# A decoder trunk's first sub-layer: both modulation rows built as rows, their slabs split between two engines, and h formed by token before plain transposes

## The chip, the cores and the metric

The kernel runs on one core of a Trainium2 chip. The metric is the device time of one execution in microseconds (us), the median of the runs. The engines are named as in the profile: PE is TensorE (PEld its weight loads), DVE is VectorE, ACT is ScalarE, POOL is GpSimd and SP is SyncE, which here issues most transfers.

## What is computed

A trunk of two layers on 256 tokens of width 1024, each layer a half-step FFN, a hybrid mixer and another half-step FFN. The change touches only the first sub-layer's input, h:

```python
mod = jax.nn.silu(c) @ w_ada[i] + b_ada[i]
sh1, sc1, g1, ... = jnp.split(mod, 9, axis=-1)
h = rms_norm(x, norm_pre[i, 0]) * (1 + sc1) + sh1
y = swiglu_ffn(h, w_ffn_in[i, 0], w_ffn_out[i, 0])
x = x + 0.5 * g1 * rms_norm(y, norm_post[i, 0])
```

`sc1` (the scale) and `sh1` (the shift) are each a product of a vector of 1024 with a 1024x1024 piece of `w_ada`, the same for every token. All arithmetic keeps fp32 accuracy: a product of two fp32 matrices is three products of their high and low parts.

## The kernel before

**Weights.** A chunk of weights is 128x1024 fp32 (512 KB). SP loads it into `w_raw` (8 buffers), ACT rounds it to `w_hi` (L1218), DVE subtracts to get `w_lo` (L1527), and PE multiplies: for each chunk of the first FFN 12 matmuls of 128x512 (L717, L718, L710), each preceded by a weight load. SP may load a chunk into a buffer once PE has used the one before (`w_used`).

**The first FFN's order.** FIRST_ORDER (L75) runs the first six chunks, numbered 0 to 5, with the first feature half of h alone (features 0 to 511, for three units of the hidden width); from chunk 6 the second half is needed. So the prologue makes h in two halves, and chunks 0 to 5 run on PE while the second half is made.

**Slabs.** `w_ada`'s pieces for scale and shift are 16 slabs of 128x1024 (`ada_slab_first`), in feature halves and loaded by SP in pairs: scale first half (signals `ada_first_landed0` to `3`), shift first half (`8` to `11`), then chunks 0 to 2, then scale second half (`4` to `7`), shift second half (`12` to `15`) with chunks 3 and 4 between, then the other chunks. A slab is used up either by DVE (a "step", L1555: accumulator plus slab times a column of silu(c), 128x512, counted in `ada_first_used`) or by PE (a matmul of the slab with that column broadcast). What DVE accumulates is 128 partial sums for each feature, with the bias in row 0; a matmul with ones sums them over the partitions and leaves the row in every partition of PSUM.

**Before, first half.** PE makes the whole scale row (L862 with ones, L866 for all 8 slabs). DVE turns it into AROW = (1 + scale) * norm_pre (L1566), multiplies x by it for each token tile (L1576) and makes a diagonal of 1/rms for each (L1666). h is then formed transposed, straight in two PSUM banks, as a sum of matmuls of 128x128 blocks: the first two shift slabs (L883), x times the diagonal (L894), and the accumulated rest of the shift times ones (L901), which waits for DVE's steps 0 to 5 on the shift. ACT rounds the result to `h_hi` (L1290), DVE subtracts to `h_lo` (L1586). PE's chunk 0 waits for `h_hi` of both token tiles and for `w_lo`.

**Before, second half.** DVE's steps 6 to 13 are the scale's 8 slabs, ended by a row of ones on PE ahead of chunk 3 (L874); steps 14 to 21 are the shift's 8 slabs. PE does the products of x with the diagonal ahead of chunk 4 and the shift's products with ones ahead of chunk 5. DVE's program between is `split_to` (the `w_lo` of a chunk) and `first_steps` in the order of L1997 to L2022.

**Beside it.** SP's load of the next sub-layer's `norm_pre` row (`pre_row`, L607) waits for `late_x`, and the bias load behind it waits until POOL has zeroed an accumulator, which waits until the second half of h is complete in PSUM (`t_ps`, L2055). Chunk 12's load stands behind both in SP's queue.

Of the kernel before, what the change touches and what calls it, by code (L numbers as in the profile page):

```python
# [11 lines left out]
ALU = mybir.AluOpType  # L12
AX_X = mybir.AxisListType.X

P = 128
D = 1024
# [251 lines left out]
def build(nc, x_d, c_d, w_ada, b_ada, norm_pre, norm_post, w_ffn_in, w_ffn_out, w_in, pool_w, w_ret_out, w_pool_out,  # L268
          w_ssm_out, w_fox_out, w_out, vecs_d, consts_d, out_d):
    with ExitStack() as ctx:  # L270
# [49 lines left out]
        DG, dg_off = sb("rstd_diagonal", [P, TT, P])  # L320
# [102 lines left out]
        first_a_ps = sem("first_half_scale_row_in_psum")  # L423
# [268 lines left out]
        def _(pe):  # L692
# [166 lines left out]
            def first_scale_row():  # L859

                pe.wait_ge(bias_landed[1].sem, bias_landed[1].at(0, 16))
                mm(PS[:, 4, :], ones, part(1)[:, 0:HALF], start=True, stop=False)  # L862
                for k in range(KD):
                    if k % 2 == 0:
                        pe.wait_ge(ada_first[k // 2], 16)
                    ins = mm(PS[:, 4, :], CS[:, k:k + 1].to_broadcast([P, P]), PSLAB[:, k, 0:HALF], start=False,  # L866
                             stop=(k == KD - 1))
                ins.then_inc(first_a_ps, 1)

            def late_scale_row():  # L870

                pe.wait_ge(first_used, FIRST_SCALE)
                pe.wait_ge(hl_ok.sem, hl_ok.at(0, 2))
                mm(PS[:, 6, :], ones, part(1)[:, HALF:D], start=True, stop=True).then_inc(a_ps.sem, 1)  # L874

            def first_pair_of_shifts():

                pe.wait_ge(ada_first[8], 16)
                pe.wait_ge(xsq_ok.sem, xsq_ok.at(0, 4))
                for tt in range(TT):  # L880
                    for k in range(4):
                        for i in range(2):
                            mm(PS[:, 6 + tt, k * P:(k + 1) * P], PSLAB[:, 8 + i, k * P:(k + 1) * P],  # L883
                               CS[:, i:i + 1].to_broadcast([P, P]), start=(k == 0 and i == 0), stop=False)

            def first_turn(half, tt):
# [5 lines left out]
                for k in range(4):  # L892
                    cs = slice(half * HALF + k * P, half * HALF + (k + 1) * P)
                    mm(PS[:, 6 + tt, k * P:(k + 1) * P], Y[:, tt, cs], DG[:, tt, :], start=(half == 1 and k == 0), stop=False)  # L894
# [1288 lines left out]
```

## Time and profile before

| | us |
|---|---|
| median of 3 runs | 1529.02 (1527.85 to 1530.41) |
| the profiled execution | 1528.89 |
| its span | 1527.1 |
| PE busy in the span | 1494.6 (98%) |
| DVE busy in the span | 1134.3 (74%) |
| granted TensorE clock, mean | 0.998 |

The span goes from the first instruction to the last, and 1.8 us of the execution lie around it. PE's share of busy time is an average: its idle time lies almost wholly in the first 50 us and in the sub-layers' boundaries. What the change touches lies in the first 55 us, so the profile is read there instruction by instruction.

### The profile page before, as it was taken

What the parts mean: (1) busy time and instruction counts of PE and PEld (TensorE: products, weight loads), DVE (VectorE), ACT (ScalarE), POOL (GpSimd) and SP (SyncE); (2) the same over time, 40 slices, a digit from 0 to 9 for tenths busy, and PEclk for the clock granted to TensorE, in tenths of its full rate; (3) what the DMA queues carried; (4) which work ended last, traced back from release to release, by engine and by line L of the source; (5) the groups of instructions that cost most, each with busy time, mean ns of one, the idle gap of its engine ahead of it and who ended that gap; (6) DMA issues with size and microseconds to landing.
All of it is one profiled execution on the core that took longest, in us unless ns stands there. A gap on an engine that the chain in (4) does not pass through costs nothing.

```text
span 1527.1 us, 20258 instructions
## 1 busy us (share of the span) xinstructions
PE 1494.6 (98%) x7904; PEld 1270.3 (83%) x7904; DVE 1134.3 (74%) x1337; ACT 780.8 (51%) x969; POOL 165.6 (11%) x96
## 2 busy tenths in 40 slices
PE   7999999999999999999999999999999999999998
PEld 4788888998988887888878888799989888878886
DVE  5887867867897988677677677767878979775453
ACT  3444455556473456444464444654746545554443
POOL 0000002203411110000000000040324012000000
PEclk9999999999999999999999999999999999999999
DMA  9899866655677856788767887565567777556652
GB/s 353 282 301 296 312 213 210 179 152 180 208 247 236 269 183 213 253 271 277 241 199 252 280 270 252 174 191 157 165 205 228 243 246 249 163 184 187 186 191 96
DMA packets 199779, 343.44 MB, mean 225 GB/s; under 512 B 18546, under 2 KB 109938, under 8 KB 199684
## 3 DMA queue, kind: packets, MB, share of 16 engines
q1 hardware_dynamic: 181540, 276.08, 57.2%
q10 hardware_dynamic: 18144, 66.07, 13.2%
q8 instruction: 62, 1.02, 0.3%
q14 instruction: 33, 0.27, 0.0%
HBM read 341.05 MB, written 1.05 MB: 224 GB/s over the span
## 4 chain that ended last, share of the span: by engine, by line
PE 83%; DVE 10%; issue 2%; ACT 2%; DMA 2%; SPq 0%; POOL 0%; ACTq 0%; DVEq 0%; POOLq 0%
PE ps L717 16%; PE ps L710 16%; PE ps L718 16%; PE ps L796 5%; PE ps L794 5%; PE ps L795 5%; PE ps L1156 4%; PE ps L1158 4%; PE ps L1157 4%; DVE w_lo L1527 2%; DVE ada_acc L1543 1%; PE ps L752 1%; DVE ada_acc L1555 1%; DMA w_raw<-in_w_ffn_in 1%; DMA ada_slab_first<-in_w_ada 1%
## 5 line engine op out<-in xcount | busy, mean ns | idle before, releaser
L1527 DVE TENSOR_TENSOR w_lo<-w_raw,w_hi 128x1024 fp32r<-128x1024 f32 x480 | 612.2, 1297 | 121.2 <-ACT w_hi L1218 120.2
L1218 ACT ACTIVATE w_hi<-w_raw 128x1024 fp32r<-128x1024 f32 x490 | 506.7, 1053 | 338.0 <-DMA w_raw<-in_w_ffn_in 114.0
L717 PE MATMUL ps<-w_hi,h_hi 128*128 128x512 f32 x1004 | 398.0, 396 | 4.2 <-DVE w_lo L1527 3.2
L718 PE MATMUL ps<-w_lo,h_hi 128*128 128x512 f32 x1004 | 391.8, 390 | 0.0
L710 PE MATMUL ps<-w_hi,h_lo 128*128 128x512 f32 x1004 | 389.8, 391 | 0.7 <-DVE h_lo L1683 0.6
L717 PEld LDWEIGHTS ps<-w_hi,h_hi 128*128 128x128 f32 x1004 | 189.0, 188 | 45.1 <-DVE w_lo L1527 4.6
L710 PEld LDWEIGHTS ps<-w_hi,h_lo 128*128 128x128 f32 x1004 | 188.3, 188 | 42.6 <-DVE h_lo L1683 2.5
L718 PEld LDWEIGHTS ps<-w_lo,h_hi 128*128 128x128 f32 x1004 | 189.1, 188 | 37.5
L1156 PE MATMUL ps<-h_hi,w_hi 128*128 128x256 f32 x704 | 201.6, 286 | 0.0
L1157 PE MATMUL ps<-h_lo,w_hi 128*128 128x256 f32 x704 | 199.1, 283 | 0.0
L1158 PE MATMUL ps<-h_hi,w_lo 128*128 128x256 f32 x704 | 199.1, 283 | 0.0
L1543 DVE SCALAR_TENSOR_TENSOR ada_acc<-ada_slab,c_silu,ada_acc 128x1024 f32<-128x1024 f32 x128 | 187.2, 1462 | 4.6 <-DMA ada_slab<-in_w_ada 4.6
L794 PE MATMUL ps<-w_hi,act_hi 128*128 128x512 f32 x352 | 137.6, 391 | 0.0
L795 PE MATMUL ps<-w_lo,act_hi 128*128 128x512 f32 x352 | 137.0, 389 | 0.0
L796 PE MATMUL ps<-w_hi,act_lo 128*128 128x512 f32 x352 | 137.0, 389 | 0.0
L1156 PEld LDWEIGHTS ps<-h_hi,w_hi 128*128 128x128 f32 x704 | 134.9, 192 | 1.6 <-DVE w_lo L1527 0.4
L1157 PEld LDWEIGHTS ps<-h_lo,w_hi 128*128 128x128 f32 x704 | 135.0, 192 | 0.3
L1158 PEld LDWEIGHTS ps<-h_hi,w_lo 128*128 128x128 f32 x704 | 135.0, 192 | 0.0
L1727 DVE TENSOR_TENSOR act_by_token<-gate_silu,ps 128x512 f32<-128x512 f32 x44 | 30.2, 687 | 133.8 <-PE ps L710 117.9
L2044 POOL MEMSET ada_acc<- 128x1024 f32 x18 | 17.0, 954 | 649.6 <-PE ps L847 601.4
L1336 ACT ACTIVATE gate_silu<-ps 128x512 f32<-128x512 f32 x44 | 26.3, 598 | 118.7 <-PE ps L710 118.7
L796 PEld LDWEIGHTS ps<-w_hi,act_lo 128*128 128x128 f32 x352 | 66.1, 188 | 13.9
(283 smaller groups left out, 1657.9 us busy)
## 6 DMA issues: line engine op xcount, KB each, us to landing
w_raw<-in_w_ffn_in SPq DMA_DIRECT2D x352, 256.0 KB, 3.6
w_raw<-in_w_in SPq DMA_DIRECT2D x168, 512.0 KB, 3.6
ada_slab<-in_w_ada ACTq DMA_DIRECT2D x126, 512.0 KB, 4.5
w_raw<-in_w_ffn_out SPq DMA_DIRECT2D x88, 512.0 KB, 4.3
ada_slab_first<-in_w_ada SPq DMA_DIRECT2D x16, 512.0 KB, 8.8
w_raw<-in_w_ssm_out SPq DMA_DIRECT2D x16, 512.0 KB, 4.4
w_raw<-in_w_out SPq DMA_DIRECT2D x16, 512.0 KB, 3.4
w_raw<-in_w_pool_out SPq DMA_DIRECT2D x8, 512.0 KB, 3.7
```

Source lines behind the costliest of these rows:

```text
L710: return mm(PS[:, banks + tt, :], lo[:, k, tok(tt)], wh[:, kk * HALF:(kk + 1) * HALF], start=False, stop=(k == kn - 1))
L717: mm(out, hi[:, k, tok(tt)], wh[:, cs], start=(k == 0), stop=False)
L718: mm(out, hi[:, k, tok(tt)], wl[:, cs], start=False, stop=False)
L794: mm(out, hi[:, k, tok(tt)], wh[:, cs], start=first, stop=False)
L795: mm(out, hi[:, k, tok(tt)], wl[:, cs], start=False, stop=False)
L796: return mm(out, lo[:, k, tok(tt)], wh[:, cs], start=False, stop=last)
L1156: mm(out, wh[:, cs], HH[:, k, :], start=(k == 0 and t % 2 == 0), stop=False)
L1157: mm(out, wh[:, cs], HL[:, k, :], start=False, stop=False)
L1158: ins = mm(out, wl[:, cs], HH[:, k, :], start=False, stop=(k == KD - 1 and t % 2 == 1))
L1218: fn(WH[:, n % N_HI, 0:width], RAW[:, n % N_RAW, 0:width], ACT.Copy).then_inc(w_hi, 1)
L1527: dve.tensor_tensor(WL[:, n % N_RAW, 0:width], RAW[:, n % N_RAW, 0:width], WH[:, n % N_HI, 0:width], ALU.subtract).then_inc(w_lo, 1)
L1543: dve.scalar_tensor_tensor(part(n), slab, CS[:, k:k + 1], part(n), ALU.mult, ALU.add)\
```

## The change

The first half's scale row is now made half by PE (slabs 0 to 3) and half by DVE (slabs 4 to 7, steps 0 to 3), with ones last. The first half's shift becomes a row as well, with DVE on slabs 0 to 3 (steps 4 to 7) and PE on slabs 4 to 7. With both rows in PSUM, DVE forms h by token, `Y = Y / rms + shift` (`first_h_full`), and PE makes 4 plain transposes for each token tile. The diagonal is gone. In the second half the scale row stays as it was; the shift row is made by DVE for slabs 0 to 5 and by PE for slabs 6 and 7, and everything that follows it (h by token, transposes) now stands ahead of chunk 6. SP's queue is as before. The core of the diff:

```diff
-FIRST_STEPS = [(1, 0, k) for k in range(2, 8)] + [(0, 1, k) for k in range(8)] + [(1, 1, k) for k in range(ADA_FIRST)]
-FIRST_SHIFT, FIRST_SCALE, LATE_SHIFT = 6, 14, 22
+FIRST_STEPS = [(0, 0, k) for k in range(4, 8)] + [(1, 0, k) for k in range(4)] + [(0, 1, k) for k in range(8)]
+FIRST_STEPS += [(1, 1, k) for k in range(6)]
+FIRST_SCALE, FIRST_SHIFT, LATE_SCALE, LATE_SHIFT = 4, 8, 16, 22
...
+            def first_row(n, half, bank, slabs, steps):
+
+                cs = slice(half * HALF, (half + 1) * HALF)
+                for k in slabs:
                     if k % 2 == 0:
+                        pe.wait_ge(ada_first[8 * n + 4 * half + k // 2], 16)
+                    mm(PS[:, bank, :], CS[:, k:k + 1].to_broadcast([P, P]), PSLAB[:, 8 * n + k, cs], start=(k == slabs[0]),
+                       stop=False)
+                pe.wait_ge(first_used, steps)
+                return mm(PS[:, bank, :], ones, part(PARTS[n])[:, cs], start=(not slabs), stop=True)
...
+                    ins = pe.transpose(PS[:, 6 + tt, k * P:(k + 1) * P], Y[:, tt, half * HALF + k * P:half * HALF + (k + 1) * P],
+                                       ident)
...
                     if s == 0 and c == 3:
-                        late_scale_row()
-                    if s == 0 and c in (4, 5):
+                        pe.wait_ge(hl_ok.sem, hl_ok.at(0, 2))
+                        first_row(0, 1, 6, (), LATE_SCALE).then_inc(a_ps.sem, 1)
+                    if s == 0 and c == 2 * EARLY:
+                        first_row(1, 1, 7, (6, 7), LATE_SHIFT).then_inc(first_rows, 1)
                         for tt in range(TT):
-                            (first_turn if c == 4 else first_shifts)(1, tt)
+                            first_turn(1, tt)
...
-            first_scale_row()
-            first_pair_of_shifts()
+            first_row(0, 0, 4, (0, 1, 2, 3), FIRST_SCALE).then_inc(first_rows, 1)
+            first_row(1, 0, 5, (4, 5, 6, 7), FIRST_SHIFT).then_inc(first_rows, 1)
+            pe.wait_ge(ident_landed, 16)
...
+            def first_h_full(half):
+
+                cs = slice(half * HALF, (half + 1) * HALF)
+                dve.wait_ge(first_rows, 2 + half)
+                for tt in range(TT):
+                    dve.scalar_tensor_tensor(Y[:, tt, cs], Y[:, tt, cs], RB[:, tt:tt + 1], PS[:, 5 + 2 * half, :], ALU.mult,
+                                             ALU.add).then_inc(late_x if half else f_ok.sem, 1)
```

On PE at the program's start, before (names: `ada_acc` is DVE's accumulator, `small_columns` holds the ones, `c_silu` the column of silu(c)):

```order
L862 MATMUL ps<-ada_acc,small_columns 128x512 [waits ada_bias_landed1,c_silu_ready,ones_ready]
L866 MATMUL ps<-ada_slab_first,c_silu 128x512 [waits ada_first_landed0]
...
L866 MATMUL ps<-ada_slab_first,c_silu 128x512 [waits ada_first_landed3]
L866 MATMUL ps<-ada_slab_first,c_silu 128x512
L883 MATMUL ps<-c_silu,ada_slab_first 128x128 [waits x_squared,ada_first_landed8]
L883 MATMUL ps<-c_silu,ada_slab_first 128x128 x15
L894 MATMUL ps<-rstd_diagonal,y_tok 128x128 [waits x_scaled_ready]
...
L901 MATMUL ps<-small_columns,ada_acc 128x128 [waits ada_first_used]
```

The same place in the changed kernel (`consts` holds the identity):

```order
L865 MATMUL ps<-ada_slab_first,c_silu 128x512 [waits ada_first_landed1]
L865 MATMUL ps<-ada_slab_first,c_silu 128x512
L868 MATMUL ps<-ada_acc,small_columns 128x512 [waits ada_first_used]
L865 MATMUL ps<-ada_slab_first,c_silu 128x512 [waits ada_first_landed10]
L865 MATMUL ps<-ada_slab_first,c_silu 128x512
L865 MATMUL ps<-ada_slab_first,c_silu 128x512 [waits ada_first_landed11]
L865 MATMUL ps<-ada_slab_first,c_silu 128x512
L868 MATMUL ps<-ada_acc,small_columns 128x512 [waits ada_first_used]
L877 MATMUL ps<-consts,y_tok 128x128 [waits x_scaled_ready,identity_landed]
L877 MATMUL ps<-consts,y_tok 128x128 x3
```

Eight slab matmuls of the scale became four, the 32 small matmuls of shift and diagonal went, and between the two rows PE now waits for the shift's last two slab pairs.

On PE around chunk 6, the changed kernel (the L710 row ends chunk 5, the L717 row begins chunk 6):

```order
L710 MATMUL ps<-w_hi,h_lo 128x512
L865 MATMUL ps<-ada_slab_first,c_silu 128x512 [waits ada_first_landed15]
L865 MATMUL ps<-ada_slab_first,c_silu 128x512
L868 MATMUL ps<-ada_acc,small_columns 128x512 [waits ada_first_used]
L877 MATMUL ps<-consts,y_tok 128x128 [waits second_half_x_scaled]
L877 MATMUL ps<-consts,y_tok 128x128 x3
L877 MATMUL ps<-consts,y_tok 128x128 [waits second_half_x_scaled]
L877 MATMUL ps<-consts,y_tok 128x128 x3
L717 MATMUL ps<-w_hi,h_hi 128x512 [waits w_lo_split,h_lo_ready]
```

Before, nothing stood between chunks 5 and 6; the second half's matmuls stood one and two chunks earlier (L894 ahead of chunk 4, L901 ahead of chunk 5).

On DVE for the same stretch, before, from the `w_lo` of chunk 4 to that of the chunks from 6 on:

```order
L1527 TENSOR_TENSOR w_lo<-w_raw,w_hi 128x1024 [waits w_hi_split]
L1555 SCALAR_TENSOR_TENSOR ada_acc<-ada_slab_first,c_silu,ada_acc 128x512 [waits ada_first_used,ada_bias_landed0,ada_first_landed14] x2
L1555 SCALAR_TENSOR_TENSOR ada_acc<-ada_slab_first,c_silu,ada_acc 128x512 [waits ada_first_used,ada_bias_landed0,ada_first_landed15] x2
L1527 TENSOR_TENSOR w_lo<-w_raw,w_hi 128x1024 [waits ada_first_used,w_hi_split]
L1586 TENSOR_TENSOR h_lo<-ps,h_hi 128x4x128 [waits h_hi_ready] x2
```

And in the changed kernel:

```order
L1506 TENSOR_TENSOR w_lo<-w_raw,w_hi 128x1024 [waits w_hi_split]
L1534 SCALAR_TENSOR_TENSOR ada_acc<-ada_slab_first,c_silu,ada_acc 128x512 [waits ada_first_used,ada_bias_landed0,ada_first_landed13]
L1534 SCALAR_TENSOR_TENSOR ada_acc<-ada_slab_first,c_silu,ada_acc 128x512 [waits ada_first_used,ada_bias_landed0,ada_first_landed14] x2
L1506 TENSOR_TENSOR w_lo<-w_raw,w_hi 128x1024 [waits ada_first_used,w_hi_split]
L1564 SCALAR_TENSOR_TENSOR y_tok<-y_tok,small_columns,ps 128x512 [waits first_rows_in_psum]
L1564 SCALAR_TENSOR_TENSOR y_tok<-y_tok,small_columns,ps 128x512
L1573 TENSOR_TENSOR h_lo<-ps,h_hi 128x4x128 [waits h_hi_ready] x2
L1506 TENSOR_TENSOR w_lo<-w_raw,w_hi 128x1024 [waits w_hi_split] x6
```

Two operations that wait for PE's new row were put in, and the `w_lo` of chunk 6 stays behind them and behind `h_lo`.

## Rows read from the trace of the kernel before

**Rows 1.** The page's first part: busy time and share of each engine.

```profile
PE 1494.6 (98%) x7904; PEld 1270.3 (83%) x7904; DVE 1134.3 (74%) x1337; ACT 780.8 (51%) x969; POOL 165.6 (11%) x96
```

**Rows 2.** Timeline, 7 to 20 us (start, duration, instruction, idle before); L866's durations.

```profile
7.83 2.04 PE L862 MATMUL ps<-ada_acc,small_columns 128*128 128x512 f32 x2 [7.83 <-DMA ada_acc<-in_b_ada]
L866 PE MATMUL ps<-ada_slab_first,c_silu x16: 592/592/1061, 9.7 to 17.4; 128*128 128x512 f32 x16
10.58 0.16 DVE L1617 SCALAR_TENSOR_TENSOR small_columns<-small_columns 128x1 f32<-128x1 f32 x1
17.67 0.75 DVE L1555 SCALAR_TENSOR_TENSOR ada_acc<-ada_slab_first,c_silu,ada_acc 128x512 f32<-128x512 f32 x1 [6.93 <-DMA ada_slab_first<-in_w_ada]
19.24 0.68 DVE L1566 SCALAR_TENSOR_TENSOR scale_row<-ps,scale_row 128x512 f32<-128x512 f32 x1
```

**Rows 3.** SP's issues (timeline), each followed by its DMA row, us to landing.

```profile
4.76 0.48 SPq L626 DMA_DIRECT2D ada_slab_first<-in_w_ada  x1
ada_slab_first<-in_w_ada SPq DMA_DIRECT2D x1, 512.0 KB, 7.5
...
5.80 0.45 SPq L632 DMA_DIRECT2D scale_row<-in_norm_pre  x1
scale_row<-in_norm_pre SPq DMA_DIRECT2D x1, 256.0 KB, 9.2
...
7.68 0.48 SPq L626 DMA_DIRECT2D ada_slab_first<-in_w_ada  x1
ada_slab_first<-in_w_ada SPq DMA_DIRECT2D x1, 512.0 KB, 11.2
...
8.21 0.79 SPq L626 DMA_DIRECT2D ada_slab_first<-in_w_ada  x1
ada_slab_first<-in_w_ada SPq DMA_DIRECT2D x1, 512.0 KB, 12.0
```

**Rows 4.** Timeline, 21 to 30 us, DVE and PE, up to chunk 0.

```profile
21.55 3.40 DVE L1555 SCALAR_TENSOR_TENSOR ada_acc<-ada_slab_first,c_silu,ada_acc 128x512 f32<-128x512 f32 x4
25.01 2.05 PE L901 MATMUL ps<-small_columns,ada_acc 128*128 128x128 f32 x16 [1.65 <-DVE ada_acc L1555]
27.75 0.50 PE L717 MATMUL ps<-w_hi,h_hi 128*128 128x512 f32 x1 [0.69 <-ACT h_hi L1290]
28.68 1.23 DVE L1527 TENSOR_TENSOR w_lo<-w_raw,w_hi 128x1024 fp32r<-128x1024 f32 x1 [0.26 <-ACT w_hi L1218]
```

**Rows 5.** Timeline, 37 to 55 us, from the second scale row to chunk 6.

```profile
37.73 1.12 PE L874 MATMUL ps<-ada_acc,small_columns 128*128 128x512 f32 x2 [0.29 <-DVE ada_acc L1555]
39.38 0.69 DVE L1566 SCALAR_TENSOR_TENSOR scale_row<-ps,scale_row 128x512 f32<-128x512 f32 x1 [0.56 <-PE ps L874]
44.63 1.22 DVE L1527 TENSOR_TENSOR w_lo<-w_raw,w_hi 128x1024 fp32r<-128x1024 f32 x1
45.90 0.50 PE L717 MATMUL ps<-w_hi,h_hi 128*128 128x512 f32 x1 [2.22 <-DVE w_lo L1527]
50.35 1.95 PE L901 MATMUL ps<-small_columns,ada_acc 128*128 128x128 f32 x16
52.96 0.69 DVE L1586 TENSOR_TENSOR h_lo<-ps,h_hi 128x512 fp32r<-128x512 f32 x1 [0.20 <-ACT h_hi L1290]
53.57 6.89 DVE L1527 TENSOR_TENSOR w_lo<-w_raw,w_hi 128x1024 fp32r<-128x1024 f32 x6
54.93 0.47 PE L717 MATMUL ps<-w_hi,h_hi 128*128 128x512 f32 x1
```

**Rows 6.** Windows: us, then PE, PEld, DVE, ACT, POOL busy, granted clock, DMA share, GB/s.

```profile
25.00:27.70 2.70, 2.05 (x16) 1.86 (x16) 1.78 (x2) 1.20 (x3) 0.00 (x0) 1.00 1.07 401
45.90:50.40 4.50, 4.50 (x13) 3.54 (x14) 3.95 (x5) 0.00 (x0) 0.00 (x0) 0.62 1.03 371
60.00:200.00 140.00, 140.00 (x639) 115.68 (x638) 114.53 (x109) 66.81 (x75) 2.87 (x3) 1.00 0.91 307
```

**Rows 7.** Timeline at 63 us: four plain transposes, of an FFN unit.

```profile
63.20 0.60 PE L752 MATMUL ps<-consts,act_by_token 128*128 128x128 f32 x4
```

More of the change, by code:

```diff
@@ L892, in first_turn @@
                 for k in range(4):
-                    cs = slice(half * HALF + k * P, half * HALF + (k + 1) * P)
-                    mm(PS[:, 6 + tt, k * P:(k + 1) * P], Y[:, tt, cs], DG[:, tt, :], start=(half == 1 and k == 0), stop=False)
-            def first_shifts(half, tt):
-                pe.wait_ge(first_used, FIRST_SHIFT if half == 0 else LATE_SHIFT)
-                for k in range(4):
-                    cs = slice(half * HALF + k * P, half * HALF + (k + 1) * P)
-                    ins = mm(PS[:, 6 + tt, k * P:(k + 1) * P], part(0)[:, cs], ones, start=False, stop=(k == 3))
+                    ins = pe.transpose(PS[:, 6 + tt, k * P:(k + 1) * P], Y[:, tt, half * HALF + k * P:half * HALF + (k + 1) * P],
+                                       ident)
                 ins.then_inc(t_ps.sem, 1)
@@ L1424, in mixer @@
                     if c == 1 and layer == 0:
+                        act.wait_ge(ident_landed, 16)
                         fn(SEL[0:32, :], ident[0:32, 0:20], ACT.Copy)
@@ L1562, in first_scale_row @@
                 if half == 0:
-                    dve.wait_ge(first_a_ps, 1)
+                    dve.wait_ge(first_rows, 1)
                 else:
@@ L1571, in first_scale_row, with first_x_scale @@
                     chain(ins)
-            def first_x_scale(half, tt):
+            def first_x_scale(half):
                 cs = slice(half * HALF, (half + 1) * HALF)
-                ins = dve.tensor_tensor(Y[:, tt, cs], X[:, tt, cs], AROW[:, cs], ALU.mult)
-                if half:
-                    ins.then_inc(late_x, 1)
+                for tt in range(TT):
+                    ins = dve.tensor_tensor(Y[:, tt, cs], X[:, tt, cs], AROW[:, cs], ALU.mult)
+                chain(ins)
+            def first_h_full(half):
+                cs = slice(half * HALF, (half + 1) * HALF)
+                dve.wait_ge(first_rows, 2 + half)
+                for tt in range(TT):
+                    dve.scalar_tensor_tensor(Y[:, tt, cs], Y[:, tt, cs], RB[:, tt:tt + 1], PS[:, 5 + 2 * half, :], ALU.mult,
+                                             ALU.add).then_inc(late_x if half else f_ok.sem, 1)
             def first_h_lo(half):
@@ L1999, in _ @@
             x_root(0, 1)
-            first_steps(0, 2)
+            first_steps(0, FIRST_SCALE)
             first_scale_row(0)
-            for tt in range(TT):
-                first_x_scale(0, tt)
-                first_diagonal(tt)
-            first_steps(2, FIRST_SHIFT)
+            first_x_scale(0)
+            first_steps(FIRST_SCALE, FIRST_SHIFT)
+            first_h_full(0)
             split_to(0)
@@ L2021, in _ @@
             split_to(5)
+            first_h_full(1)
             first_h_lo(1)
```

41 lines of the change are left out of this document (7 added, 34 removed).

## The prediction

> **What bounds the kernel now.** I read the page's first part, then the timeline of the first 55 us, then windows for the stretch behind it. PE is busy 98% of the span [rows 1] and without a gap from 60 to 200 us [rows 6], so once chunk 6 starts, a shift of its start moves everything behind it by as much. The question is when chunk 6 starts: 54.93 us before [rows 5]. Up to there PE is not the bound. Four places set the pace: the first shift slabs' landing, for which DVE idled 6.93 us [rows 2]; h_hi ahead of chunk 0, at 27.75 [rows 4]; DVE's chain of steps and w_lo, which released chunk 4 at 45.90 after PE had idled 2.22 us; and chunk 4, the shift's products (50.35) and chunk 5, back to back on PE, up to 54.93 [rows 5].
>
> **The unit prices.** A DVE step starts 0.88 us behind the one before (4 steps in 3.40 us [rows 4], one alone 0.75 [rows 2]). A w_lo takes 1.15 us of DVE's time (6 in 6.89) [rows 5]. An fp32 matmul of 128x512 is two passes: two passes to the end of the result took 1.12 us at the high clock [rows 5] and 2.04 us at the low one [rows 2], hence, with the drain taken off, about 0.43 and 0.86 us a pass. A chunk takes 2.8 us at the high clock: chunk 5 lies between L901's end, drain taken off (52.1), and 54.93 [rows 5].
>
> **Part 1, the scale row of the first half.** x's roots are done at 10.74 [rows 2]. DVE then runs four steps; the last slab pair landed at 4.76 + 7.5 = 12.3 us [rows 3], so they end between 14.2 and 15.0. PE has 8 passes from about 7.9, the first ones slow as before, and waits; the ones take 1.12. AROW's own input lands at 5.80 + 9.2 = 15.0 [rows 3]. The scale row's DVE operation starts at about 15.6, instead of 19.24 [rows 2]: 3.6 us earlier, since it no longer stands behind two steps that wait for slabs. The x products follow (1.3 us) and four steps on the shift (3.5), done by about 21.
>
> **Part 2, the shift row, where that gain goes.** PE's half of the shift is slabs 4 to 7, the last to arrive: 7.68 + 11.2 = 18.9 and 8.21 + 12.0 = 20.2 us [rows 3]. From 18.9 it has 8 slab passes and 2 of ones, 4.3 us at the high clock, with a short wait for the last pair: done at 23.4. But PE has stood idle from about 15.4 to 18.9. In the trace, chunk 4 came after 2.22 us of idle time [rows 5] and ran with a granted clock of 0.62 over 4.5 us [rows 6], that is, 3.4 us at the low level (1.2 GHz) and the rest at 2.4; 1.65 us of idle time ahead of L901 [rows 4] did not lower it (1.00 afterwards) [rows 6]. An idle time of 3.5 us is beyond the row that lowered it, so I take the low clock and its 3.4 us: 1.7 us lost, shift row done at 25.2. The bounds are 23.4 and, were all 10 passes slow, 27.5.
>
> Then DVE forms h of both tiles (0.3 to see the row, the nearest rows being 0.1 and 0.5; 0.69 and 0.6 for two operations such as L1566 [rows 5]), done at 26.8; 4 transposes take 0.60 [rows 7]; ACT's h_hi ends at 28.1. Chunk 0 starts at 28.15, against 27.75 [rows 4]: +0.4 (bounds: -1.4 and +2.7). Taking out the diagonal and 32 small matmuls is free, since PE waits there for DVE or slabs anyway.
>
> **Part 3, DVE's chain to chunk 4.** The w_lo of chunk 1 starts 0.45 later than 28.68. Up to the w_lo of chunk 4 the chain was DVE's: 12 steps, three more w_lo, the scale row and two products, and it ended at 45.85. Now it has 11 steps (-0.88) and one wait for the last product (+0.1): 45.5, a gain of 0.35. The products of x with the diagonal ahead of chunk 4 are gone from PE, which is worth nothing: PE waited 2.22 us behind them [rows 5], and now waits some 3.5. Chunk 4 therefore runs at the low clock as before (4.45 us, 45.90 to 50.35) and ends at 49.95, chunk 5 at 52.75.
>
> **Part 4, ahead of chunk 6.** Before, the shift's products cost PE 1.70 us on the path, and all that followed them (h_hi, h_lo, the w_lo of chunk 6) ran beside chunk 5. Now the row stands behind chunk 5 and covers nothing:
> - 2 slabs and the ones: 6 passes and the drain, 2.85 us, to 55.6;
> - DVE sees it and forms h of both tiles: 1.6, to 57.2;
> - 4 transposes of the second tile: 0.65, to 57.85;
> - from there to PE's release, as from L901's end (52.30) to 54.85 in the trace, h_hi, h_lo and the w_lo of chunk 6: 2.55 [rows 5], to 60.4.
> Against 54.93 chunk 6 starts **5.5 us later**. The w_lo of chunks 6 on stood in the same queue before, behind h_lo; they were merely hidden.
>
> **Part 5, the clock behind it.** Of 55.6 to 60.4 PE works 1.2 us at most, on transposes, and then idles 2.5 us at a stretch. By the row with 2.22 us the clock falls: 3.4 us at the low level cost 1.7 more. The other bound is nothing, by the row with 1.65 us.
> Of transposes the traces before show no case of their own. The Trainium skill ("TensorE: Matmul & The Clock Gate", Part 4: PE-mode transpose) says that transposes do not count as busy for the clock. Its rule makes the idle stretch longer and the fall surer; without it I would take the same value with less weight.
>
> **Part 6, queues.** late_x now comes from h by token, so SP's norm_pre row, the bias and then chunk 12's load are issued near 59 instead of 53.6, some 1.3 us nearer to chunk 6 than before. Chunk 12 is wanted 16 us after chunk 6; that room hides it, and costs nothing. POOL's zeroing moves along.
>
> **The sum.** +5.5 and +1.7 on the profiled execution's 1528.89, which lies at the median of the runs (1529.02): **1536.1**.
>
> **The rivals.**
> 1. One of the two new low stretches fails to come (the clock depends on where the idle time falls, and either place has two stretches of work near it). Without the one behind chunk 5: 1534.4. Without the one in the shift row the start moves by -1.8, and all behind it: 1534.3.
> 2. Neither comes: 1532.6. For it speaks only that 1.65 us were harmless; against it, that both gaps are above 2.22.
> 3. Not slower: the clock stays high in chunk 4 too. It decides there: if the new 3.5 us gap ahead of chunk 4 falls so that the clock does not drop, or drops after chunk 5, the old loss of 1.7 us goes as well, and with rival 2 the sum is 5.5 - 1.8 - 1.7 = +2.0: 1530.9, within 0.2%. Against it: chunk 4's gap grows.
> 4. The low clock lasts longer: all ten passes of the shift row (+2.3), or also chunk 5 (+1.4): 1538.
> 5. The change doesn't hold chunk 6 back at all, because the second half's row is made while PE waits for chunk 4's w_lo. PE runs its program in order and the row stands behind chunk 5, and DVE's last steps end at about 48: it can't, unless the order is not what it reads. It would give the start's -0.35 and the 1.7 of the shift's products: 1526.8.
>
> **The numbers.** Forecast 1536.1 with 0.47; rival 1 0.26; rival 2 0.08; rival 3 0.07; rival 4 0.09; rival 5 0.03. The range takes in rivals 1 and 2 and most of 4: 1532.3 to 1538.2. About 0.2% (3.06 us) is what a measurement of this kernel tells from no change. Slower by more than that: the forecast, rivals 1 and 4, most of rival 2: 0.86. Within: 0.11. Faster: 0.03.
>
> **What would show it.** In the changed kernel's timeline: the first scale row's DVE operation near 15.6; a PE gap up to 18.9, then slab passes with a granted clock near 0.5 to 0.6; chunk 0 at 28.2 (26.4 if that clock is high); chunk 4 near 45.5; the second shift row ending near 55.6, and PE's next L717 near 60.4, with a low granted clock in the 3 us behind it. I am wrong if chunk 6 starts before 58, if the shift row isn't the last input of chunk 0, or if PE is idle again between 60 and 200 us, which would let a later start be made up.

## The result, and the profile after

The changed kernel takes **1540.20 us** (median of 4 runs, 1538.75 to 1544.68), the kernel before in the same comparison 1528.43 us (4 runs, 1527.28 to 1530.41). The ratio is 1.0081, with a 95% interval of 1.0070 to 1.0093: slower. A second comparison gave 1537.95 against 1528.14, 1.0060 (1.0043 to 1.0077). The profiled execution is one of 1538.75 us with a span of 1536.9.

The page's first part for the changed kernel (busy us, share, records of each engine) answers to [rows 1]. PE has 72 records fewer (a record is one pass of a matmul, and an fp32 matmul has two), and as many weight loads fewer. That looked like nothing, and is what the second half of this text is about.

```profile
PE 1495.6 (97%) x7832; PEld 1265.1 (82%) x7832; DVE 1135.7 (74%) x1339; ACT 781.6 (51%) x969; POOL 165.6 (11%) x96
```

Timeline of the changed kernel, 13 to 28 us, PE and DVE up to chunk 0; it answers to [rows 2, 4]:

```profile
15.93 0.69 DVE L1545 SCALAR_TENSOR_TENSOR scale_row<-ps,scale_row 128x512 f32<-128x512 f32 x1 [1.29 <-PE ps L868]
...
18.43 5.40 PE L865 MATMUL ps<-ada_slab_first,c_silu 128*128 128x512 f32 x8 [2.62 <-DMA ada_slab_first<-in_w_ada]
...
23.67 1.02 PE L868 MATMUL ps<-ada_acc,small_columns 128*128 128x512 f32 x2
...
24.73 1.40 DVE L1564 SCALAR_TENSOR_TENSOR y_tok<-y_tok,small_columns,ps 128x512 f32<-128x512 f32 x2 [3.34 <-PE ps L868]
...
27.53 0.50 PE L717 MATMUL ps<-w_hi,h_hi 128*128 128x512 f32 x1 [0.69 <-ACT h_hi L1268]
```

Timeline of the changed kernel, 43 to 60 us, from chunk 4's `w_lo` to chunk 6; it answers to [rows 5]:

```profile
43.70 1.22 DVE L1506 TENSOR_TENSOR w_lo<-w_raw,w_hi 128x1024 fp32r<-128x1024 f32 x1
44.98 0.50 PE L717 MATMUL ps<-w_hi,h_hi 128*128 128x512 f32 x1 [2.87 <-DVE w_lo L1506]
...
51.68 1.88 PE L865 MATMUL ps<-ada_slab_first,c_silu 128*128 128x512 f32 x4
...
53.39 1.02 PE L868 MATMUL ps<-ada_acc,small_columns 128*128 128x512 f32 x2
...
54.45 1.41 DVE L1564 SCALAR_TENSOR_TENSOR y_tok<-y_tok,small_columns,ps 128x512 f32<-128x512 f32 x2 [5.72 <-PE ps L868]
55.25 1.31 PE L877 MATMUL ps<-consts,y_tok 128*128 128x128 f32 x8 [0.84 <-DVE y_tok L1564]
56.58 1.35 DVE L1573 TENSOR_TENSOR h_lo<-ps,h_hi 128x512 fp32r<-128x512 f32 x2 [0.72 <-ACT h_hi L1268]
...
59.20 0.47 PE L717 MATMUL ps<-w_hi,h_hi 128*128 128x512 f32 x1 [2.63 <-DVE w_lo L1506]
```

Windows of the changed kernel (columns as in [rows 6]; the seventh is the granted clock, 1.00 for 2.4 GHz): the shift row of the first half, chunk 4, and the stretch behind chunk 6's start.

```profile
20.00:25.00 5.00, 4.69 (x8) 1.64 (x6) 1.53 (x3) 1.06 (x1) 0.00 (x0) 0.69 1.07 396
44.00:48.00 4.00, 3.01 (x12) 2.17 (x12) 3.59 (x5) 0.00 (x0) 0.00 (x0) 1.00 1.08 384
60.00:64.00 4.00, 4.00 (x12) 3.14 (x11) 4.00 (x5) 3.98 (x5) 0.00 (x0) 0.59 0.76 234
```

The chain that the prediction described is there, row for row. Chunk 6 starts at 59.20 instead of 54.93 [rows 5], and the low clock behind it makes that 5.9 us at the first transposes of an FFN unit (69.11 instead of 63.20 [rows 7]). But the span grew by 9.8 us (1536.9 against 1527.1). The other 4 us came far behind the prologue, at the boundaries between sub-layers: 2.2 of them near 600 us. In the changed kernel ACT waits longer there for the load of a weight chunk, then PE for what ACT and DVE make behind that. ACT's row and PE's row of the kernel before near 600 us:

```profile
601.09 1.06 ACT L1218 ACTIVATE w_hi<-w_raw 128x1024 fp32r<-128x1024 f32 x1 [3.53 <-DMA w_raw<-in_w_ffn_in]
...
604.90 0.66 PE L752 MATMUL ps<-consts,act_by_token 128*128 128x128 f32 x4 [1.44 <-DVE act_by_token L1727]
```

The same two of the changed kernel:

```profile
609.03 1.06 ACT L1196 ACTIVATE w_hi<-w_raw 128x1024 fp32r<-128x1024 f32 x1 [5.20 <-DMA w_raw<-in_w_ffn_in]
...
612.85 0.66 PE L752 MATMUL ps<-consts,act_by_token 128*128 128x128 f32 x4 [2.02 <-DVE act_by_token L1709]
```

That longer idle time is 0.6 of the 2.2 us. The rest is a fall of the clock that came ahead of both rows, behind an idle time of PE that is shorter than at the same place before (1.36 against 1.65 us); the changed kernel's row, and its window behind it:

```profile
598.49 1.32 PE L835 MATMUL ps<-consts,y_tok 128*128 128x128 f32 x8 [1.36 <-DVE y_tok L1656]
600.00:604.00 4.00, 4.00 (x11) 3.15 (x12) 4.00 (x5) 3.40 (x4) 0.00 (x0) 0.57 0.09 15
```

### The profile page after: what moved, and what is told of

It reads as the page before. It is cut to its first block, busy times and chain, and to the rows that moved or that the text cites. A ratio compares the mean times of both kernels' runs of the same rounds, so it can differ in the third digit from the quotient of the medians.

```text
span 1536.9 us, 20118 instructions
## 1 busy us (share of the span) xinstructions
PE 1495.6 (97%) x7832; PEld 1265.1 (82%) x7832; DVE 1135.7 (74%) x1339; ACT 781.6 (51%) x969; POOL 165.6 (11%) x96
## 4 chain that ended last, share of the span: by engine, by line
PE 81%; DVE 11%; issue 3%; ACT 2%; DMA 2%; SPq 0%; POOL 0%; ACTq 0%; DVEq 0%; POOLq 0%
PE ps L717 16%; PE ps L710 15%; PE ps L718 15%; PE ps L795 5%; PE ps L796 5%; PE ps L794 5%; PE ps L1135 4%; PE ps L1137 4%; PE ps L1136 4%; DVE w_lo L1506 2%; DVE ada_acc L1522 1%; PE ps L752 1%; DMA w_raw<-in_w_ffn_in 1%; DVE x_res L1631 1%; DVE y_tok L1640 1%
## 5 line engine op out<-in xcount | busy, mean ns | idle before, releaser
L717 PE MATMUL ps<-w_hi,h_hi 128*128 128x512 f32 x1004 | 399.4, 398 | 8.2 <-DVE w_lo L1506 7.2
L710 PE MATMUL ps<-w_hi,h_lo 128*128 128x512 f32 x1004 | 391.0, 392 | 0.1
L717 PEld LDWEIGHTS ps<-w_hi,h_hi 128*128 128x128 f32 x1004 | 189.6, 189 | 50.2 <-DVE w_lo L1506 6.6
L710 PEld LDWEIGHTS ps<-w_hi,h_lo 128*128 128x128 f32 x1004 | 189.2, 189 | 42.2 <-DVE h_lo L1665 1.7
```

Of the source, the lines that this page charges most:

```text
L710: return mm(PS[:, banks + tt, :], lo[:, k, tok(tt)], wh[:, kk * HALF:(kk + 1) * HALF], start=False, stop=(k == kn - 1))
L717: mm(out, hi[:, k, tok(tt)], wh[:, cs], start=(k == 0), stop=False)
```

## The experiments

All ratios are against the kernel before, run in the same comparison, with 95% intervals.

### Is a later start of chunk 6 passed on in full?

The kernel before with useless fp32 matmuls of 128x512 between chunks 5 and 6 (N is 2, 4, 7 and 9):

```diff
+                    for _ in range(N):
+                        mm(PS[:, 6, :], ones, X[:, 0, 0:HALF], start=True, stop=True)
```

> The kernel before with 2 useless fp32 matmuls of 128x512 (ones times x, 4 passes) on PE between chunks 5 and 6: a pure delay of 1.7 us of all that follows, with PE busy. Theory A (what is lost ahead of chunk 6 is passed on one to one and nothing else happens): +1.7 us on the kernel before, mean granted clock as before (0.998). Theory B (the place in time of the later gaps decides whether PE's clock falls there, so that a mere shift can cost several us more): +1.7 and 0 to 6 us more, the surplus with a lower mean clock.

> The same with 4 useless matmuls: a delay of 3.4 us. Theory A: +3.4 us, clock as before. Theory B: +3.4 plus a surplus that differs from those of the delays of 1.7 and 6.0 us; since each low stretch in both traces lasts 3.4 us, the smallest surplus of the three is expected here.

> The same with 7 useless matmuls: a delay of 6.0 us, as much as the changed kernel lost up to 70 us. Theory A: +6.0 us, clock 0.998. Theory B: about what the changed kernel shows against before, +9 to +12, with a mean clock of 0.991 to 0.995.

> The kernel before with 9 useless matmuls between chunks 5 and 6, a delay of 7.7 us with PE busy, by which boundary gaps fall at the times at which they fall in the changed kernel. If the changed kernel's low-clock stretches behind 590 us come from where the gaps fall: +10 us or more with a mean clock of 0.996 or less. If not: +6.5 to +8 us, clock 0.998 or more.

| N | PE's added work, us | median, us | less before's | ratio |
|---|---|---|---|---|
| 2 | 1.7 | 1530.22 | +2.1 | 1.0011 (1.0001 to 1.0020) |
| 4 | 3.5 | 1532.22 | +4.1 | 1.0022 (1.0012 to 1.0031) |
| 7 | 6.1 | 1532.76 | +4.6 | 1.0032 (1.0021 to 1.0043) |
| 9 | 7.9 | 1536.00 | +7.8 | 1.0046 (1.0032 to 1.0060) |

(The added work is N times 0.877 us, from the last one's row of 18 records in 7.89 us.) Over the four, a delay in front of chunk 6 is passed on: the total is within 0.6 us of it for three and 1.5 us under it for N = 7, whose mean clock was the highest of the four (0.9989, the others 0.9972 to 0.9975). Nothing behind it adds to it, and the surplus of theory B did not come. So the changed kernel's +9.8 to +11.8 needs more than its prologue. That its time is real and no accident of one comparison:

> The changed kernel once more, beside the delays on the same chip. Both theories: +10 to +13 us on the kernel before with a mean clock of 0.991 to 0.995; by theory B its executions differ by their clock, 1 to 2 us for each 0.001 of it.

Measured: 1537.95 us, 1.0060 (1.0043 to 1.0077), +9.8 us, just under what was expected. Three of its four executions have a mean clock of 0.992 to 0.996; the fourth is listed with 0.944 and is the second fastest, so that reading is not used.

### Which half of the change costs what?

The second half's edit alone, on before's first half (the `late_shift_row` and the transposes ahead of chunk 6):

```diff
-                    if s == 0 and c in (4, 5):
+                    if s == 0 and c == 2 * EARLY:
+                        late_shift_row()
                         for tt in range(TT):
-                            (first_turn if c == 4 else first_shifts)(1, tt)
+                            late_turn(tt)
```

> Half of the change alone: the first half of h as before, the second half's shift as a row with h by token and transposes ahead of chunk 6. Theory 1 (the loss is the serial row, h, transposes, h_hi, h_lo and w_lo between chunks 5 and 6): chunk 6 starts near 60 us and is followed by a low-clock stretch, +7 to +11 us on the kernel before, as much as the whole change. Theory 2 (the first half's PE idle time and its low clock carry a good part of the loss): +3 to +5 us.

Measured: 1535.22 us, 1.0040 (1.0026 to 1.0055), +7.0 us, the low end of theory 1; chunk 6 at 60.34, behind the same idle time of 2.63 us.

The first half's edit alone, with before's second half (products with the diagonal ahead of chunk 4, the shift's ahead of chunk 5):

```diff
-                    if s == 0 and c == 2 * EARLY:
-                        first_row(1, 1, 7, (6, 7), LATE_SHIFT).then_inc(first_rows, 1)
+                    if s == 0 and c in (4, 5):
                         for tt in range(TT):
-                            first_turn(1, tt)
+                            (late_turn if c == 4 else late_shifts)(tt)
```

> The other half alone: both rows, h by token and transposes for the first half, the second half as before (all 8 shift slabs on DVE, products with the diagonal and with ones ahead of chunks 4 and 5). Theory 1: chunk 0 near 27.5, chunk 6 within 1 us of before, and the time within 1.5 us of the kernel before. Theory 2: +3 to +6 us.

Measured: 1529.16 us, 1.0001 (0.9990 to 1.0011), and chunk 6 at 54.16, 0.8 us earlier than before, without a gain in the total. The second half's edit carries the loss. The first half's, which starts chunk 6 earlier, should have gained and doesn't: its ten executions have a mean granted clock of 0.996, the kernel before's 0.998.

A rebuilt version keeps the first half by rows and takes the second half's row off the path: four slabs each on DVE and PE, PE's ahead of chunk 4 and the ones ahead of chunk 5, h by token beside chunk 5, the transposes ahead of chunk 5's last product, and chunk 6's `w_lo` ahead of `h_lo`.

```diff
+                    if s == 0 and c == 4:
+                        late_slabs((4, 5))
+                        late_slabs((6, 7))
+                    if s == 0 and c == 5:
+                        pe.wait_ge(first_used, LATE_SHIFT)
+                        mm(PS[:, 7, :], ones, part(0)[:, HALF:D], start=False, stop=True).then_inc(first_rows, 1)
```

> The changed kernel with its second half put where PE has room: slabs 4 to 7 of the shift on PE ahead of chunk 4 (DVE keeps 4 slabs), the row of ones ahead of chunk 5, the transposes inside chunk 5, and chunk 6's w_lo ahead of h_lo. Theory 1: the serial stretch is covered by chunk 5, PE is never idle for long behind 42 us, chunk 6 starts at 53 to 54 us: -2 to 0 us on the kernel before. Theory 2: +3 or more remains.

Measured: 1531.53 us, 1.0017 (1.0006 to 1.0028), although chunk 6 starts at 51.82, 3.1 us before it does in [rows 5]. The mechanism of the prologue was mended and the time was still above before's; again the mean clock was 0.996. Something in the two kernels with the first half by rows costs time far from it: by the median and the start of chunk 6 in the profiled execution, some 2 us in the first half's edit alone and some 6 in this one.

### The low clock

The changed kernel with three matmuls that add nothing (the stationary operand is zero) in the idle time ahead of chunk 6:

```diff
+                        for _ in range(3):
+                            mm(PS[:, 4, :], DA[:, 0, 0:1].to_broadcast([P, P]), X[:, 0, 0:HALF], start=False, stop=False)
```

> The changed kernel with three more fp32 matmuls of 128x512 on PE behind the second half's transposes and ahead of chunk 6. Their stationary operand is zero and they go into a bank that the units accumulate in, so they add nothing; PE would have idled there for 2.63 us behind h_hi, h_lo and the w_lo. Theory A, the low clock behind chunk 5 comes from that idle time: PE's idle time ahead of chunk 6 shrinks to under 0.3 us, chunk 6 starts within 0.2 us of where it did (59.2), the granted clock of 60 to 64 us is 1.00 instead of low, and the time falls by 1.7 us against the changed kernel, to about 1536.3 in these comparisons (ratio to the kernel before 1.005). Theory B, the clock falls there for another reason: it is low again between 60 and 64 and the time stays near 1538.

Timeline and window of that kernel: the filling leaves no idle time ahead of chunk 6, which starts where it did, and the clock stays high.

```profile
56.51 2.74 PE L905 MATMUL ps<-x_res,da 128*128 128x512 f32 x6
...
59.30 0.47 PE L717 MATMUL ps<-w_hi,h_hi 128*128 128x512 f32 x1
```

```profile
60.00:64.00 4.00, 4.00 (x20) 3.26 (x19) 4.00 (x5) 3.98 (x5) 0.00 (x0) 1.00 0.80 252
```

Twenty matmuls instead of twelve in the same 4 us, as by theory A. The time was 1536.93, 1.0044 (1.0031 to 1.0058), where 1.005 was expected. The same filling also in the gap between the first half's two rows:

```diff
             first_row(0, 0, 4, (0, 1, 2, 3), FIRST_SCALE).then_inc(first_rows, 1)
+            for _ in range(3):
+                mm(PS[:, 7, :], ones, PSLAB[:, 0, 0:HALF], start=True, stop=True)
```

> As the run before, and three more such matmuls (ones against a slab, into a bank that is written anew later) between the first scale row (done at 15.8) and the first shift slab that PE waits for (18.4). Theory A: the low stretch of the first shift row goes too, chunk 0 starts at 25.9 instead of 27.5, and the time is 3.4 us below the changed kernel's, near 1534.6; if the number of later low stretches follows from the early ones it may be lower still. Theory B, later low stretches are drawn anew in each execution and have nothing to do with the prologue: the mean clock rises only by the two early stretches. Theory C, the first stretch is low whatever PE did before: chunk 0 stays at 27.3 to 27.5.

Its trace has the shift row's slabs in 3.70 us instead of 5.40 and chunk 0 at 26.19 instead of 27.53. Its median, 1535.77 (1534.6 was expected), 1.0049 (1.0037 to 1.0062), is no better than that of the run before within the intervals, and the mean clock is 0.996 in both. So the fillings do what they should where they stand, and the clock far behind does not follow them.

Is it the first half by rows that brings the later low clock? Before's first half with the rebuilt version's second half (the diff is against the second half's edit alone), and the rebuilt version with the first gap filled, by the lines just shown:

```diff
-                    if s == 0 and c == 2 * EARLY:
+                    if s == 0 and c == 4:
+                        late_slabs((4, 5))
+                        late_slabs((6, 7))
+                    if s == 0 and c == 5:
                         late_shift_row()
-                        for tt in range(TT):
-                            late_turn(tt)
```

> The kernel before's first half with another second half: the shift as a row, four slabs on DVE and four on PE ahead of chunk 4, its row of ones ahead of chunk 5, h by token beside chunk 5, and the transposes ahead of that chunk's last product, with the w_lo of chunk 6 ahead of h_lo. If the extra low stretches that the kernels with the first half by rows showed far behind the prologue come from that first half, this one has a mean clock like the kernel before's (0.998 and more); chunk 6 starts near 52.5 to 53.5 and the time is 1526.5 to 1528, ratio 0.999 to 1.000. If they come with any second half that is early or by rows, it has them too: a mean clock of 0.995 to 0.997 and 1529 to 1531.

> The rebuilt version (both halves by rows, the second half as in the run before) with the three matmuls in the gap between the first scale row and the first shift slabs. With the first stretch at the high clock in each execution chunk 0 starts at 25.7 in each and chunk 6 near 51.8. If the early idle time of 3.5 us is what brings the later low stretches, the mean clock rises to 0.998 and more and the time falls to 1526 to 1527.5, below the kernel before; if the later ones are drawn independently, the time is at most 1 us under the 1531.5 of the rebuilt version.

Measured: 1527.76 us, 0.9995 (0.9986 to 1.0003), mean clock 0.9985 and chunk 6 at 53.43, for the first; 1531.22 us, 1.0014 (1.0005 to 1.0022), mean clock 0.9961, for the second. The extra loss goes with the first half by rows, and not with its idle time, which the second kernel doesn't have. What else goes with it is the number of PE's records: 14 fewer than before in the first of these two, 62 in the second, 54 and 68 in the first half's edit alone and the rebuilt version.

### What the boundaries show

The DMA view of one stretch lists the queues at work in it. For the kernel before, from SP's issue of the loads behind the boundary near 600 us (595.79) to ACT's use of the chunk (601.09); columns: queue and kind, packets, MB, share of 16 DMA engines:

```profile
q1 hardware_dynamic: 806, 0.78, 43.4%
q10 hardware_dynamic: 144, 0.52, 36.0%
```

The same stretch of the changed kernel (602.71 to 609.03):

```profile
q1 hardware_dynamic: 1147, 1.11, 54.4%
q10 hardware_dynamic: 144, 0.52, 27.5%
q8 instruction: 1, 0.02, 0.9%
```

One packet is more there, of the queue that loads instructions. The page lists that queue for the whole span:

```profile
q8 instruction: 62, 1.02, 0.3%
```

62 packets of 16 KB. PE has 7904 records of matmuls and 7904 of weight loads in the kernel before, 15808 instructions, and 15808 / 62 is 255: one packet for each 255 or so of PE's instructions. The Trainium skill ("Runtime: NRT & Kernel Launch", Instruction fetch mechanics) says that an engine's instructions are refilled in blocks of 16 KiB, 256 instructions, and that the cost is mostly hidden. The trace agrees on the size. Whether the cost is hidden is what is at stake here, and not for PE's own fetching but for a load that is under way beside it.

**Where** these packets fall is set by the number of PE instructions ahead. The changed kernel has 2 x 72 = 144 fewer, more than half a block. Narrow windows place the first packet at 31.3 us before and at 48.8 after, and near the boundary at 575.2 and 609.7 before, 570.6 and 603.4 after.

The 18 traces of this study (two are of the changed kernel) can be sorted by whether a packet starts in the flight of the chunk's two loads, from the first issue to the landing of the second. Each range is over the traces of its row:

| boundary near | packet | traces | second load, issue to landing, us | ACT's wait, us |
|---|---|---|---|---|
| 600 us | outside | 12 | 4.49 to 4.78 | 3.36 to 3.62 |
| 600 us | inside | 6 | 5.49 to 6.05 | 4.63 to 5.20 |
| 800 us | outside | 10 | 4.41 to 4.75 | 3.26 to 4.20 |
| 800 us | inside | 8 | 5.11 to 5.99 in six, 4.62 in two | 4.56 to 4.85, and 3.48 and 4.10 |
| 1345 us | outside | 12 | 3.13 to 3.30 | 2.02 to 2.15 in ten, 2.62 and 2.70 |
| 1345 us | inside | 6 | 4.30 to 4.66 in five, 3.39 in one | 3.16 to 3.52, and 2.87 |

The three exceptions inside are of the changed kernel: in one trace the packet starts 0.65 us ahead of the landing near 800 us, in the other about 0.2 us behind the second issue, near 800 and 1345 us (two flights near 600 us with a packet as early were lengthened). So a packet in the flight lengthens it in 17 of 20 cases, and no flight without one is as long. (The four kernels with a pure delay have no packet in any of the three flights.) ACT's wait has a second cause. In all six traces whose wait is long though the flight is not (4.01 to 4.20 us in four near 800 us, 2.62, 2.70 and 2.87 us near 1345 us, one trace in both), the clock had fallen behind the idle time of PE just ahead, and the loads, which wait until PE has used a buffer, were issued 0.9 to 1.3 us later behind it than in the others.

### The number of instructions alone

If this is the cause, it can be had without the change, and undone with it. Four kernels get matmuls of one element at the start, where PE waits for its first load until 7.8 us; nothing else in them is touched. In the kernel before this adds 112 instructions, which puts the packets as far ahead in PE's program as 144 fewer do, since 112 + 144 is one block of 256; in the others it restores the count of the kernel before (N is 28 in the kernel before, 36 in the changed one, 34 in the rebuilt one, 31 in the rebuilt one with the first gap filled):

```diff
             pe.wait_ge(one_ok, 1)
+            for _ in range(N):
+                mm(PS[0:1, 3, 0:1], one, one, start=True, stop=True)
```

> The kernel before with 28 matmuls of one element (56 records, with their loads 112 instructions) on PE at the start, where it idles until 7.8 us; nothing else is changed. The instruction transfers (62 of 16 KB, one for each 256 of PE's instructions) then come as far ahead in PE's program as in the changed kernel, which has 72 records (144 instructions) fewer. Theory A, these transfers delay the first chunk load behind a boundary when they fall between its issue and its landing: the transfers move into these stretches (near 597, 790 and 1343 us, where the kernel before has none), ACT's wait for the chunk grows from 3.5, 3.6 and 2.05 us to 4.6 to 5.0 or 2.7 to 3.5 at two or three of them, PE idles 2.5 us and more at some, the mean clock falls to 0.994 to 0.997, and the median rises by 1 to 3 us, to 1530 to 1532. Theory B, the first half by rows does it in another way: time and clock stay the kernel before's (0.998), within 0.5 us.

> The changed kernel with 36 matmuls of one element (72 records) on PE at the start, so that PE's instructions are as many as before's. Theory A: the instruction transfers lie as in the kernel before, clear of the chunk loads at the boundaries; ACT's waits there are 3.4 to 3.6 and near 2.05 us, the mean clock rises to 0.997 to 0.998 and the median falls by 1.5 to 3 us against the changed kernel (1.006 to 1.008), to a ratio of 1.0045 to 1.0055, the prologue's loss alone. Theory B: no change, 1.006 to 1.008.

> The rebuilt version with 34 matmuls of one element (68 records) at the start, so that PE's instructions are as many as before's. Theory A: mean clock 0.998, the median 2 to 4 us under the 1531.5 of the rebuilt version, 1527 to 1529, ratio 0.999 to 1.000. Theory B: 1531 to 1532.

> The rebuilt version with the three filling matmuls in the first gap and 31 matmuls of one element at the start. Theory A: chunk 6 starts near 51.8 in each execution and the instruction transfers lie as before: mean clock 0.998 to 0.999, 1526 to 1527.5, ratio 0.998 to 0.999, the fastest of all. Theory B: 1531.

| kernel | PE records | median, us | ratio | without the small matmuls |
|---|---|---|---|---|
| before, shifted | 7960 | 1531.93 | 1.0018 (1.0009 to 1.0027) | 1 |
| changed, shifted | 7904 | 1536.62 | 1.0044 (1.0031 to 1.0056) | 1.0081 (1.0070 to 1.0093), 1.0060 (1.0043 to 1.0077) |
| rebuilt, shifted | 7904 | 1529.09 | 1.0001 (0.9992 to 1.0009) | 1.0017 (1.0006 to 1.0028) |
| rebuilt and filled, shifted | 7904 | 1527.09 | 0.9990 (0.9981 to 0.9999) | 1.0014 (1.0005 to 1.0022) |

The first row decides whether the count alone can cost time. The small matmuls of the shifted kernel before cost nothing where they stand, as its timeline shows (PE still waits 5.39 us behind them, for the same DMA):

```profile
1.09 1.54 PE L1191 MATMUL ps<-small_columns 128*1 128x1 f32 x56 [1.09 <-DVE small_columns L1996]
8.02 1.19 PE L862 MATMUL ps<-ada_acc,small_columns 128*128 128x512 f32 x1 [5.39 <-DMA ada_acc<-in_b_ada]
```

And yet it is 2.6 us slower. Its DMA view from issue to use at the boundary near 600 us (595.61 to 601.99):

```profile
q8 instruction: 1, 0.02, 0.9%
```

Its timeline there, with the packet at 599.5, shows how one packet becomes idle time of PE:

```profile
595.61 6.49 SPq L570 DMA_DIRECT2D w_raw<-in_w_ffn_in  x8
...
601.99 1.06 ACT L1220 ACTIVATE w_hi<-w_raw 128x1024 fp32r<-128x1024 f32 x1 [4.64 <-DMA w_raw<-in_w_ffn_in]
...
603.07 1.28 ACT L1338 ACT_TABLE_LOAD   x1
...
604.37 0.60 ACT L1338 ACTIVATE gate_silu<-ps 128x512 f32<-128x512 f32 x1
...
605.07 0.69 DVE L1729 TENSOR_TENSOR act_by_token<-gate_silu,ps 128x512 f32<-128x512 f32 x1 [3.03 <-ACT gate_silu L1338]
...
605.81 0.66 PE L752 MATMUL ps<-consts,act_by_token 128*128 128x128 f32 x4 [2.51 <-DVE act_by_token L1729]
```

Read it from the top: in ACT's program the rounding of this chunk stands ahead of the gate's activation, so the load holds back the gate, the gate holds back DVE's product, and PE idles 2.51 us instead of 1.44. Behind that the clock fell. The windows of the stretch behind it in the kernel before, and in the shifted one:

```profile
606.00:610.00 4.00, 4.00 (x20) 3.27 (x19) 4.00 (x5) 1.51 (x2) 0.00 (x0) 1.00 0.94 323
```

```profile
606.00:610.00 4.00, 4.00 (x14) 3.18 (x14) 4.00 (x5) 2.29 (x3) 0.00 (x0) 0.57 0.90 320
```

The same chunk's landing in the chain that ended last (start, us), for the kernel before:

```profile
596.38 4.69 DMA w_raw<-in_w_ffn_in
```

for it shifted, then for the changed kernel, and for the changed kernel shifted:

```profile
596.19 5.78 DMA w_raw<-in_w_ffn_in
```

```profile
603.29 5.72 DMA w_raw<-in_w_ffn_in
```

```profile
601.86 4.59 DMA w_raw<-in_w_ffn_in
```

4.6 to 4.7 us without the packet, 5.7 to 5.8 with it, whether the kernel is the old one or the new one. The shifted kernel before has its packet in the flight at all three boundaries, and PE idles 2.51, 2.51 and 1.03 us behind them, where it idled 1.44, 1.48 and less than 0.1 us without. The rebuilt version moves the other way with the same small matmuls, by 2.4 us, and with the first gap filled by 4.1, there with intervals that don't touch; so they are not themselves the cost.

The changed kernel's eight executions lie at 1.0055 or more of the kernel before's median in their comparison, and the five of the shifted one at 1.0050 or less, so that one gained too. Two of the expectations on the clock were missed: the changed kernel, shifted, has a mean of 0.995 (0.997 to 0.998 was expected) and the rebuilt one, shifted, 0.9965 (0.998). Their traces have low stretches that no packet explains, behind idle times of PE of 1.4 us. The last kernel of the table has chunk 0 at 25.69, chunk 6 at 51.81 and ACT's wait near 600 us back at 3.62:

```profile
51.81 0.50 PE L719 MATMUL ps<-w_hi,h_hi 128*128 128x512 f32 x1 [0.88 <-DVE h_lo L1593]
```

It is faster than both kernels, than the one before by 0.1%, with an interval that ends just short of no change.

## Why the prediction was wrong, point by point

The forecast was 1536.1 us and the measured median 1540.20, above its range; the direction was right. (The second comparison's 1537.95 lies inside the range.) The step that failed is a term put at nothing: that taking 72 records out of PE's program is free. The sum of the prologue's terms was about right.

- **Part 1** held. The scale row's DVE operation starts at 15.93 (forecast 15.6) instead of 19.24 [rows 2].
- **Part 2** held and was 0.6 us too high. PE's slabs began at 18.43, the clock fell (0.69 in the mean from 20 to 25 us), the row was done at 24.7 (25.2) and chunk 0 started at 27.53 (28.15).
- **Part 3**, the clock of chunk 4, failed in the profiled execution. It came at 44.98 (45.5) behind 2.87 us of idle time and ran at the high clock (1.00 from 44 to 48 us), where [rows 6] had 0.62 behind 2.22 us. The repeated run of the same kernel had it low again, and of the kernels with before's second half some had it low and some not. So an idle time of 2.2 to 3.2 us there lets the clock fall in some executions only (and once 1.90 us did, in the first half's edit alone). The row was one draw, and "Chunk 4 therefore runs at the low clock as before" read a rule out of it.
- **Part 4** held to 0.2 us. From chunk 5's end to chunk 6 it is 51.7 to 59.20, 7.5 us; the terms forecast 2.85 + 1.6 + 0.65 + 2.55 = 7.65. Measured one by one: 2.7, 1.45, 0.70 and 2.64. Against [rows 5] chunk 6 moved by 4.27 and not 5.5, because chunk 4 came 0.5 us earlier and was fast. The high clock there was worth 0.6 us and not 1.7, since PE then idled 0.79 us ahead of chunk 5.
- **Part 5** held: 0.59 in the mean from 60 to 64 us, and gone when the idle time was filled.
- **Part 6** is where the step is missing. SP's three issues moved to 55.88, 56.26 and 57.90 (forecast: near 59), and PE has no gap of over 0.5 us between 60 and 200 us, so they cost nothing, as forecast. But the part lists only the queues that the program fills. The queue of PE's own instructions is not in it, though its row is on the page of the kernel before. Taking out 72 records was booked in part 2 as costing nothing ("free, since PE waits there"). It moved the first instruction packet by 17.5 us, and the later ones into the loads behind the boundaries. What that does was measured on the kernel before by a count that puts the packets as far ahead: +2.6 us.

With the instruction count restored, the changed kernel is at 1.0044 (1.0031 to 1.0056) of before, that is +6.7 us (+4.7 to +8.6) in that comparison. The forecast's +7.2 lies inside, and the prologue of the profiled execution, +5.9 us at 69 us, lies 1.3 under it. So the sum of the prologue's terms had about the right size. The rest of the measured +9.8 to +11.8, some 3 to 5 us, is gone when the instruction count is restored. That share is a difference between comparisons and is known to a microsecond or two only: against the second comparison of the changed kernel, 1.0060, the intervals overlap. Not all of it is traced to a packet. In the profiled execution a packet was in the flight at all three boundaries and lengthened it at two, and of two low stretches far out, 1.7 us each, one (613.6 us) came behind the lengthened idle time and the other (600.0 us) ahead of the packet, behind 1.36 us of idle time. Why that one came is open.

The rivals: none named it. Rival 4 (a longer low clock) came nearest in time, for another reason; the low stretches that came were new ones, far behind the prologue. Half of rival 3's condition, chunk 4 at the high clock, did occur in the profiled execution, but the two new low stretches came as well. The sign "if PE is idle again between 60 and 200 us" looked for what would give time back; that time could be lost further out was not looked for.

**What stays open.** How a 16 KB packet holds back the chunk's landing by 1.1 us was not tried; its share, 0.9% of 16 engines over 6.3 us, is 0.9 us of one DMA engine, which would fit if the chunk's last packets stood behind it on that engine. The three flights that a packet did not lengthen are not explained. Nor is it settled which idle times lower the clock. In the 18 traces, behind 70 us and up to the last boundary, it fell behind 7 of the 10 idle times of 1.9 to 2.8 us ahead of the transposes that a gate feeds (all ten with the packet in the flight), and behind none of the 31 of 0.7 to 1.6 us at that place. But it also fell behind 17 of the 90 idle times of 1.36 to 1.65 us at the sub-layers' starts, in kernels with and without a packet near. Whether the packets' position has a part in these was not tried.

## What to carry to other kernels

Count the instructions that an edit adds to or takes from a busy engine, even where they cost no time, and look where that engine's instruction packets fall against the loads that someone waits for at once. When an edit's effect is a few microseconds and does not match its mechanism, run the kernel before with as many idle-time dummies as make the counts equal: it separates the edit from its shift of the program. And a serial chain that was moved behind the work which used to cover it costs its whole length: here 7.5 us between chunks 5 and 6 where 1.7 us of it stood on the path before, forecast from single rows to 0.2 us, and mended by slabs ahead of chunk 4 and h beside chunk 5.

## What the runs showed of the hardware

- One packet of 16 KB in the queue of PE's instructions, in the flight of a weight chunk that is waited for at once, made the chunk land 1.1 us later (5.78 instead of 4.69 us from issue to landing). In the kernel before, where nothing but the count of instructions was changed, it did so at three boundaries, and the median rose by 2.6 us of 1529.
- PE's clock fell for 3.4 us (once for 6.8) behind idle times of 2.2 to 3.2 us ahead of chunk 4 in some traces and not in others, for the changed kernel in one of two. It fell behind 17 of 90 idle times of 1.36 to 1.65 us at the sub-layers' starts too, so that the prediction's "1.65 us were harmless" held for its row only.
- Three fp32 matmuls in the idle time kept the clock up where this was tried: ahead of chunk 6 in two traces of two (low in all four traces of kernels with that idle time unfilled), and ahead of the first shift row in three of three (low in six of seven unfilled).
- 28 matmuls of one element (56 records) took 1.54 us, inside PE's idle time at the start. That idle time ended at 8.02 us, against 7.7 to 8.6 in the traces of kernels without them.
